# Layer A's cache copies one by one in the attention stages, and GpSimd's subtraction ahead of the next pair's weight sums

## The chip, the cores and the metric

The kernel runs on one core of one Trainium2 chip. The metric is the device time in microseconds (us), the median of the runs of one program. All data are float32 and lie in HBM before and after.

## The reference, cut to what matters

One inference step of a decoder trunk of two layers, for a prompt group (1024 tokens) and a sample group (8 sequences of 4 new tokens). Layer A, the first, multiplies the normalised input by one wide matrix `w_in_a` and runs dilated window attention in three groups, 4 heads each, beside attention into 256 memory tokens; layer B is a gated DeltaNet. The sample group keeps caches: of each group's keys and values the oldest 4 tokens are dropped where the window is full, and the 4 new ones appended. For the change only this counts:

```python
kc = jnp.concatenate([kbuf, k], axis=1)
vc = jnp.concatenate([vbuf, v], axis=1)
keep = min(win, L + T)
return o, lse, kc[:, L + T - keep:], vc[:, L + T - keep:]
```

So most of each new cache is a plain copy of the old one. For groups 1 and 2 (512 cached tokens, 4 heads of 128) these are four tensors, k and v of each, with 8 sequences of about 1 MB.

## The kernel before, in words

**Tasks.** The projection of layer A is made in 24 pairs of 128-column blocks of `w_in_a` (`SIDES`, six pairs for each of 4 heads). A pair is worked off by two tasks, one for each part of the tokens (`SUBS`: 272 and 256 columns), so there are 48 tasks; task t belongs to pair t // 2, and odd tasks are a pair's second half. A task is seven products of eight matmuls (`product`, L878): a scheme that gets four block products out of seven, from sums and differences of weights and of tokens. The weights' sums are made by GpSimd, four for each pair (`weight_sums(pair, ns)`, L1314, 128x512 each): the first overwrites half of the right block by left minus right, the second gives wS2, the third wS4, the fourth wS1. TensorE waits for the second ahead of a task's third product (i = 2), for the third ahead of i = 3, for the fourth ahead of i = 6. ScalarE and VectorE read the products out of PSUM (`evacuate`: L1046, L1049, L1052, L1062, L1065 on ScalarE, L1134, L1140, L1144, L1152, L1155 on VectorE). Between VectorE's step of i = 3 and its last step, i = 6 (L1152), GpSimd subtracts once for each task (L1334, `beside` with i = 4), and VectorE's last step waits for that (`pr_pool`).

**Weights.** Blocks of 128 columns, 512 KB each, lie in a ring of four slots (`Ring`, L136), two pairs. SyncE loads a block when the slot's old block is used up (`ring.used`), that is after the pair before last. TensorE waits for a pair's two loads ahead of its first product, GpSimd ahead of its first sum.

**Stages.** Behind the first four tasks (0 to 3) come 16 attention stages, s = 4h + g for head h and group g (g = 3 is the memory attention). Each stage has steps of its own: transposes (L915), scores (L930), transposed probabilities and values (L951, L954), softmax on VectorE (L1171, L1176, L1182, L1183) and ScalarE (L1087). The matmuls of three tasks are laid between them by `segments()`, in fixed shares: stage s has tasks 3s + 4 to 3s + 6, as far as there are any. All engines follow the same written order (`ended`, `stage_ends`). At stage g = 3 GpSimd also combines the three groups (`combined`, L1345 to L1349), called behind `beside` of task 12h + 14, i = 4.

**GpSimd's order.** For an odd task it issues the first three sums of the next pair at i = 3, the subtraction of the running task at i = 4, and the fourth sum at i = 6; for an even task only the subtraction. GpSimd works in order, so each waits for what stands ahead.

**Cache copies.** `copy_cache` (L302) issues four transfers from HBM to HBM on GpSimd's software queue, for two sequences each (2032 KB, or 2 MB where nothing is dropped). It is called at the start of stages 0, 4, 8 and 12, for one tensor each: 16 transfers in layer A's attention (L305). Eight small ones of group 0 come behind layer A (L2947). Only the end of the kernel waits for them all (L3101). Beside them SyncE issues the weight loads, the stores of new keys and values (L793 to L798), and the way of the groups' partial outputs to HBM and back (L814 to L821), all on the hardware queue.

Of the kernel before, what the change touches and what calls it, by code (L numbers as in the profile page):

```python
# [18 lines left out]
NB, DT = 8, 4  # L19
# [86 lines left out]
def after(eng, sem, value):  # L106

    if not isinstance(value, int) or value > 0:
        eng.wait_ge(sem, value)
# [34 lines left out]
def build(nc, ins, outs):  # L144
# [46 lines left out]
    NPAIR = len(SIDES) * H  # L191
# [107 lines left out]
    const_tp, const_sp, tab_in, mats_in = (nc.alloc_semaphore(n) for n in ("const_tp", "const_sp", "tab_in", "mats_in"))  # L299
    NTAB = 3 + H  # L300

    def copy_cache(pool, src, dst, n, drop):  # L302

        for b in range(0, NB, 2):
            pool.dma_start(dst[0, b:b + 2, 0:n - drop].rearrange("b t h e -> b (t h e)"),  # L305
                           src[0, b:b + 2, drop:n].rearrange("b t h e -> b (t h e)")).then_inc(copies, 16)
    NCOPY = 6 * NB // 2


    def part_in(k, part_):  # L310
# [54 lines left out]
    def tables_copied(pool):  # L365

        pool.wait_ge(tab_out, 32)
        pool.dma_start(toep, toep_rows.unsqueeze(1).to_broadcast([3 * H, P, 3 * P])).then_inc(tab_copied, 16)

    def sample_tables_in(pool):  # L370

        nc.gpsimd.memset(b2[:, :, :], NEG).then_inc(b2_set, 1)
        for h in range(H):
            pool.dma_start(bias_s[h * NS:(h + 1) * NS].rearrange("p g c -> p (g c)"),
                           sampb[h].unsqueeze(0).to_broadcast([NB, DT, 6 * P])).then_inc(tab_in, 16)

    def tables_in(pool):

        pool.wait_ge(b2_set, 1)
        pool.wait_ge(tab_copied, 16)  # L380
        pool.dma_start(b01[:, :, :], bass.AP(toep.tensor, P - 1, [[3 * P - 1, P], [P * 3 * P, 2 * H], [1, 256]])
                       ).then_inc(tab_in, 16)
        for r in range(2):
            pool.dma_start(b2[64 * r:64 * r + 64, :, 64 * r:64 * r + 64],
                           bass.AP(toep.tensor, 2 * H * P * 3 * P + 63,
                                   [[3 * P - 1, 64], [P * 3 * P, H], [1, 64]])).then_inc(tab_in, 16)
# [4 lines left out]
    @block.sync  # L391
    def _(sp):
        def x_load(n):
            sp.dma_start(xs[0:rows_in(n), n], load_in(n)).then_inc(x_in[n], 16)

        sp.dma_start(mats[:, 0:1, :], c_mats[:, 0:P].rearrange("p (m c) -> p m c", c=P)).then_inc(id_in, 16)
        x_load(XT)
        x_load(XT + 1)
        ring.load(sp, 2)
        sp.wait_ge(ring.loaded[0], 16)  # L400
        x_load(0)
        sp.dma_start(wb, norm_w[0].unsqueeze(0).to_broadcast([P, D])).then_inc(w_in, 16)
        x_load(1)
        ring.load(sp, 3)
        sp.wait_ge(rel_set, 1)
        sp.dma_start(relx[0:NBUCKET, :], rel_bias).then_inc(rel_in, 16)
        sp.dma_start(c_tp, c_toep).then_inc(const_tp, 16)
        x_load(2)
        x_load(3)
        ring.load(sp, 4)  # L410
        sp.dma_start(c_sp, c_samp).then_inc(const_sp, 16)
        x_load(4)
        x_load(5)
        ring.load(sp, 5)
        x_load(6)
        x_load(7)
        x_load(8)
        ring.load(sp, NMB + 2)
        sp.dma_start(mats[:, 1:, :], c_mats[:, P:].rearrange("p (m c) -> p m c", c=P)).then_inc(mats_in, 16)
        ring.load(sp, NMB + RING)  # L420
        sp.wait_ge(ev_a, 2)
        sp.wait_ge(ev_v, 2)
        sp.dma_start(memT_kept, memT_in).then_inc(memT_out, 16)
        sp.wait_ge(mem_tev, 8)
        mem_rows_out(sp, 0)
# [203 lines left out]
    for n in range(NPRE, len(loads)):  # L629
        a, i, kv = loads[n]  # L630
# [659 lines left out]
    @block.gpsimd  # L1290
    def _(pool):
        own = Chain(nc, pool, "pool_a")

        def weight_sums(pair, ns):

            x = (B0 + 2 * pair) % RING
            left, right = ring.slots[:, x, :, :], ring.slots[:, x + 1, :, :]
            before = NPROD * (2 * pair - 1)
            for n in ns:
                if n == 0:  # L1300
                    ring.wait(pool, B0 + 2 * pair)
                    ring.wait(pool, B0 + 2 * pair + 1)
                    v = right[:, 0:KH, :], left[:, 0:KH, :], right[:, 0:KH, :], ALU.subtract
                elif n == 1:
                    after(pool, pr_done, before + 3)
                    v = wS2, right[:, KH:KD, :], right[:, 0:KH, :], ALU.subtract
                elif n == 2:
                    after(pool, pr_done, before + 4)
                    v = wS4, left[:, KH:KD, :], wS2, ALU.subtract
                else:  # L1310
                    after(pool, pr_done, before + 7)
                    v = wS1, wS2, left[:, 0:KH, :], ALU.add
                after(pool, w_sums, 4 * pair + n)
                nc.gpsimd.tensor_tensor(*v).then_inc(w_sums, 1)  # L1314

        def token_rest(half):

            lo, hi = SUBS[half]
            pool.wait_ge(tok_sums, 2 * half + 2)
            v = hT[:, 0:KH, HALF + lo:HALF + hi]  # L1320
            nc.gpsimd.tensor_tensor(v, v, hT[:, 0:KH, lo:hi], ALU.subtract).then_inc(tok_rest, 1)
            four = lambda y: y.rearrange("p (a b) c -> p a b c", b=2)
            nc.gpsimd.tensor_tensor(tok_f[:, :, :, lo:hi], four(hT[:, KH:KD, lo:hi]), four(tok_e[:, :, lo:hi]),
                                    ALU.subtract).then_inc(tok_rest, 1)

        def beside(t, i):

            pair, n = t // 2, SUBS[t % 2][1] - SUBS[t % 2][0]
            if i == 3 and t % 2 and pair + 1 < NPAIR:
                weight_sums(pair + 1, (0, 1, 2))  # L1330
            if i == 4:
                pool.wait_ge(pr_dve, 4 * t + 2)
                pool.wait_ge(pr_act, 4 * t + 3)
                nc.gpsimd.tensor_tensor(w1s1[:, 0:n], w1s1[:, 0:n], u3[:, 0:n], ALU.subtract).then_inc(pr_pool, 1)  # L1334
            if i == 6 and t % 2 and pair + 1 < NPAIR:
                weight_sums(pair + 1, (3,))

        def combined(h):

            pool.wait_ge(comb_w, 2 * h + 2)  # L1340
            after(pool, t_read, EBASE[4] * h)
            if not h:
                pool.wait_ge(mem_out, 32)
            w = lambda g: wcomb[:, 2, g * NT:(g + 1) * NT].unsqueeze(2).to_broadcast([P, NT, E])
            own(nc.gpsimd.tensor_tensor(ocomb[:, :, :], og[0][:, :, 0:E], w(0), ALU.mult))  # L1345
            own(nc.gpsimd.tensor_tensor(og[1][:, :, 0:E], og[1][:, :, 0:E], w(1), ALU.mult))
            own(nc.gpsimd.tensor_tensor(og[2][:, :, 0:E], og[2][:, :, 0:E], w(2), ALU.mult))
            own(nc.gpsimd.tensor_tensor(ocomb[:, :, :], ocomb[:, :, :], og[1][:, :, 0:E], ALU.add))
            nc.gpsimd.tensor_tensor(ocomb[:, :, :], ocomb[:, :, :], og[2][:, :, 0:E], ALU.add).then_inc(comb_o, 1)  # L1349

        weight_sums(0, range(4))
        tables_copied(pool)
        pool.wait_ge(tab_row, 9)
        token_rest(0)
        pool.wait_ge(normed, NT + 1)
        token_rest(1)
        sample_tables_in(pool)
        for t, i in ALL_FIRST:
            beside(t, i)
            if (t, i) == (1, 4):  # L1360
                tables_in(pool)
        for s in range(NSTAGE):
            h, g = s // 4, s % 4
            if g == 0:
                copy_cache(pool, *((ck1, sk1, 512, DT), (cv1, sv1, 512, DT), (ck2, sk2, 512, 0),
                                   (cv2, sv2, 512, 0))[h])
            for t, i in stage_ends(s):
                beside(t, i)
                if g == 3 and (t, i) == (12 * h + 14, 4):
                    combined(h)  # L1370
            if s == NSTAGE - 1:
                pool.wait_ge(sc_read, 8 * (NSTAGE - 1))
                for v in Z_small:
                    own(nc.gpsimd.memset(v, 0.0))
                for g in (0, 2):
                    own(nc.gpsimd.tensor_copy(spread(0, g), gathered(0, g, q_of[0](g))))
                combined(h)
        pool.wait_ge(comb_o, H)
        own(nc.gpsimd.memset(Z_wide, 0.0))
# [1672 lines left out]
    def _(sp):  # L3052
# [46 lines left out]
        for i, d in enumerate(dso):  # L3099
            sp.wait_ge(d, 16 * len(range(i, NQ, 3)))  # L3100
        sp.wait_ge(copies, 16 * NCOPY)  # L3101
        sp.wait_ge(en, 1)
# [539 lines left out]
```

## Time and profile before

| | |
|---|---|
| median of 3 runs | 2256.55 us (2255.39 to 2259.75) |
| the profiled execution | 2256.22 us, its span 2254.3 us |
| TensorE busy | 2158.5 us, 96% |
| VectorE, ScalarE, GpSimd busy | 934.9, 663.6, 455.5 us |
| layer A's attention stages | about 112 to 862 us |
| mean granted clock of TensorE | 0.985 of full speed |

Times in the trace count from the span's start. A wait is put down to what ended it; "issue" is a wait that ended by no instruction that the profile shows, a transfer's landing among them. "SPq" is SyncE's queue of DMA issues. PEld is TensorE's loading of weights, which runs beside its matmuls.

### The profile page before, as it was taken

How to read it: one execution, taken by the hardware profiler on the slowest of the kernel's cores; microseconds unless marked ns; L12 is line 12 of the kernel's file. 1: busy time of each engine (PE TensorE's matmuls, PEld its weight loads, DVE VectorE, ACT ScalarE, POOL GpSimd, SP SyncE). 2: the span in 40 equal slices, each digit the busy share in tenths (PEclk: the TensorE clock that was granted, in tenths of full speed). 3: DMA queues.
4: the chain of work that ended last, by engine and by line, in shares of the span. 5: the costliest groups of instructions: out<-in, count | busy, mean ns of one | idle time of the engine just before them, and what ended most of it. 6: DMA issues, size and time to landing. Idle time of an engine off the chain costs nothing. (4 is left out here: it accounts for less than half of the span.)

```text
span 2254.3 us, 46735 instructions
## 1 busy us (share of the span) xinstructions
PE 2158.5 (96%) x19630; PEld 1533.0 (68%) x19630; DVE 934.9 (41%) x2431; ACT 663.6 (29%) x1589; POOL 455.5 (20%) x642
## 2 busy tenths in 40 slices
PE   8999988996999699999999999999999999999998
PEld 6888867885888587554466676766766766665444
DVE  5243443342435244331235555555556323333252
ACT  3122211311131123221133444444444344452101
POOL 0521232131223121400032123223222010010000
PEclk9999998998999899999999999999999999999999
DMA  7442232215132327657411011001001141015451
GB/s 225 154 182 82 57 141 76 76 38 189 29 85 86 132 67 223 230 179 237 150 29 31 3 31 32 22 12 32 22 3 41 29 166 57 19 45 170 132 175 53
DMA packets 210278, 210.99 MB, mean 94 GB/s; under 512 B 14262, under 2 KB 181654, under 8 KB 209151
## 3 DMA queue, kind: packets, MB, share of 16 engines
q1 hardware_dynamic: 198070, 148.27, 22.0%
q0 software_dynamic: 12000, 59.73, 7.0%
q8 instruction: 158, 2.59, 0.5%
q14 instruction: 50, 0.40, 0.1%
HBM read 179.56 MB, written 68.23 MB: 110 GB/s over the span
## 5 line engine op out<-in xcount | busy, mean ns | idle before, releaser
L878 PE MATMUL bank<-arena 128*128 128x256 f32 (+1 forms) x2688 | 635.2, 387 | 58.0 <-issue 58.0
L878 PEld LDWEIGHTS bank<-arena 128*128 128x128 f32 x2688 | 496.0, 191 | 134.5 <-issue 59.1
L2083 PE MATMUL bank<-arena 128*128 128x352 f32 x1296 | 468.9, 473 | 0.1
L2083 PEld LDWEIGHTS bank<-arena 128*128 128x128 f32 x1296 | 213.8, 190 | 58.1 <-ACT arena L2304 0.6
L1314 POOL TENSOR_TENSOR arena<-arena 128x512 f32<-128x512 f32 x96 | 122.8, 1279 | 308.2 <-PE bank L878 162.5
L2795 PE MATMUL bank<-arena 128*128 128x352 f32 x576 | 176.4, 459 | 0.0
L3283 PE MATMUL bank<-arena 128*128 128x512 f32 x360 | 167.5, 599 | 0.0
L2141 PEld LDWEIGHTS bank<-arena 128*128 128x128 f32 x864 | 125.1, 191 | 36.7 <-issue 0.3
L2795 PEld LDWEIGHTS bank<-arena 128*128 128x128 f32 x576 | 106.6, 190 | 53.3
L2157 PEld LDWEIGHTS bank<-arena 32*32 32x32 f32 x7680 | 78.6, 105 | 87.4 <-issue 35.4
L2141 PE MATMUL bank<-arena 128*128 128x128 f32 x864 | 130.8, 277 | 0.2 <-ACT arena L2324 0.2
L1654 PE MATMUL bank<-arena 128*128 128x512 f32 x248 | 122.1, 607 | 1.7 <-DMA arena<-in_w_out_a 1.7
L2440 DVE SCALAR_TENSOR_TENSOR arena<-arena 128x512 f32<-128x512 f32 x144 | 116.0, 806 | 1.2
L3283 PEld LDWEIGHTS bank<-arena 128*128 128x128 f32 x360 | 64.4, 189 | 70.4 <-issue 70.4
L2157 PE MATMUL bank<-arena 32*32 32x16 f32 (+1 forms) x7680 | 96.5, 183 | 1.1 <-DVE arena L2526 0.7
L1152 DVE TENSOR_TENSOR arena<-bank,arena 128x272 f32<-128x272 f32 (+1 forms) x48 | 24.2, 504 | 162.9 <-POOL arena L1334 87.8
L915 PE MATMUL bank<-arena 128*128 128x128 f32 x396 | 79.9, 278 | 8.4 <-ACT arena L1087 7.2
L1334 POOL TENSOR_TENSOR arena<-arena 128x272 f32<-128x272 f32 (+1 forms) x48 | 31.3, 652 | 269.2 <-ACT arena L1052 245.9
L1160 DVE COPY arena<-bank 128x256 f32<-128x256 f32 (+1 forms) x208 | 78.7, 383 | 13.9 <-PE bank L915 13.9
L1087 ACT ACTIVATE arena<-arena 128x256 f32<-128x256 f32 (+1 forms) x128 | 59.7, 467 | 83.3 <-DVE arena L1176 76.3
L915 PEld LDWEIGHTS bank<-arena 128*128 128x128 f32 x396 | 53.7, 143 | 30.4 <-ACT arena L1087 8.4
L2705 POOL TENSOR_TENSOR arena<-arena 128x512 f32<-128x512 f32 x16 | 21.1, 1321 | 252.2 <-DVE arena L2480 252.2
(426 smaller groups left out, 2717.9 us busy)
## 6 DMA issues: line engine op xcount, KB each, us to landing
arena<-in_w_in_a SPq DMA_DIRECT2D x48, 512.0 KB, 5.6
arena<-in_w_in_b SPq DMA_DIRECT2D x40, 512.0 KB, 3.8
arena<-in_cache_win_k SPq DMA_DIRECT2D x48, 256.0 KB, 5.0
arena<-in_cache_win_v SPq DMA_DIRECT2D x48, 256.0 KB, 3.6
out<-arena SPq DMA_DIRECT2D x40, 256.0 KB, 3.4
arena<-in_w_mem_kv SPq DMA_DIRECT2D x16, 512.0 KB, 8.1
arena<-in_cache_mem_k SPq DMA_DIRECT2D x32, 256.0 KB, 4.0
arena<-in_cache_mem_v SPq DMA_DIRECT2D x32, 256.0 KB, 3.7
```

The costliest lines, as they stand in the source:

```text
L878: m = nc.tensor.matmul(o[:, 0:hi - lo], w, y, start=k == 0 and i in (0, 1, 3, 5), stop=k == KH - 1, skip_group_check=i in (2, 4, 6))
L915: m = nc.tensor.transpose(tB[e % 2][:, c * P:(c + 1) * P], src, ident)
L1087: nc.scalar.activation(pr[:, x % 2, c:256], sS[:, x % 2, c:256], ACT.Exp, bias=nm, accum_out=l).then_inc(p_done, 1)
L1160: nc.vector.tensor_copy(dst, tB[e % 2][:, lo:lo + w]).then_inc(t_read, 1)
L1314: nc.gpsimd.tensor_tensor(*v).then_inc(w_sums, 1)
L1654: i = nc.tensor.matmul(bank[BY0 + half][:, :], brT[:, k, n * P:(n + 1) * P], wo_a(k)[:, half * 512:(half + 1) * 512], start=j == 0, stop=j ...
L2083: m = nc.tensor.matmul(bank[j % 3][:, 0:PART], ring.slots[:, (B1 + b) % RING, k, :], part_in(k, part_), start=k == 0, stop=k == KD - 1)
L2141: m = nc.tensor.matmul(o[:, c * P:(c + 1) * P], l, r, start=True, stop=True)
L2157: m = nc.tensor.matmul(o[quarter(i), lo:lo + r.free_size()], l, r, start=True, stop=True)
L2440: x = nc.vector.scalar_tensor_tensor(out=dst, in0=src, scalar=cw, in1=dst, op0=ALU.mult, op1=ALU.add)
L2795: m = nc.tensor.matmul(bank[part_][:, 0:PART], ring.slots[:, (B2 + b) % RING, k, :], part_in(k, part_), start=k == 0, stop=k == KD - 1)
L3283: m = nc.tensor.matmul(bank[BY0 + half][:, :], brT[:, k, n * P:(n + 1) * P], wo_b(k)[:, half * 512:(half + 1) * 512], start=j == 0, stop=j ...
```

## The change

`copy_cache` takes the list of sequences. A new helper, `copy_part(pool, n)`, issues the n-th of the 16 transfers alone (n // 4 is the tensor, n % 4 the pair of sequences). The four calls at the starts of stages 0, 4, 8 and 12 are gone. Transfers 14 and 15 are issued in the first tasks, behind `beside(2, 4)` and `beside(3, 4)`; transfers 0 to 13 in stages 0 to 13, behind `beside(3 * s + 5, 4)`, the middle task of each stage. In `beside`, the first three sums of the next pair move from i = 3 to i = 4, behind the running task's subtraction. What is computed, and the bytes that are copied, are the same.

```diff
-    def copy_cache(pool, src, dst, n, drop):
-
-        for b in range(0, NB, 2):
+    def copy_cache(pool, src, dst, n, drop, bs=range(0, NB, 2)):
+
+        for b in bs:
             pool.dma_start(dst[0, b:b + 2, 0:n - drop].rearrange("b t h e -> b (t h e)"),
                            src[0, b:b + 2, drop:n].rearrange("b t h e -> b (t h e)")).then_inc(copies, 16)
     NCOPY = 6 * NB // 2
+
+    def copy_part(pool, n):
+
+        src, dst, drop = ((ck1, sk1, DT), (cv1, sv1, DT), (ck2, sk2, 0), (cv2, sv2, 0))[n // 4]
+        copy_cache(pool, src, dst, 512, drop, (n % 4 * 2,))
...
         def beside(t, i):
 
             pair, n = t // 2, SUBS[t % 2][1] - SUBS[t % 2][0]
-            if i == 3 and t % 2 and pair + 1 < NPAIR:
-                weight_sums(pair + 1, (0, 1, 2))
             if i == 4:
                 pool.wait_ge(pr_dve, 4 * t + 2)
                 pool.wait_ge(pr_act, 4 * t + 3)
                 nc.gpsimd.tensor_tensor(w1s1[:, 0:n], w1s1[:, 0:n], u3[:, 0:n], ALU.subtract).then_inc(pr_pool, 1)
+                if t % 2 and pair + 1 < NPAIR:
+                    weight_sums(pair + 1, (0, 1, 2))
             if i == 6 and t % 2 and pair + 1 < NPAIR:
                 weight_sums(pair + 1, (3,))
...
             beside(t, i)
             if (t, i) == (1, 4):
                 tables_in(pool)
+            if (t, i) in ((2, 4), (3, 4)):
+                copy_part(pool, 12 + t)
         for s in range(NSTAGE):
             h, g = s // 4, s % 4
-            if g == 0:
-                copy_cache(pool, *((ck1, sk1, 512, DT), (cv1, sv1, 512, DT), (ck2, sk2, 512, 0),
-                                   (cv2, sv2, 512, 0))[h])
             for t, i in stage_ends(s):
                 beside(t, i)
+                if (t, i) == (3 * s + 5, 4) and s < 14:
+                    copy_part(pool, s)
                 if g == 3 and (t, i) == (12 * h + 14, 4):
                     combined(h)
```

## Rows read from the trace of the kernel before

**Rows 1.** The page: busy time, share of the span and instructions of each engine.
```profile
PE 2158.5 (96%) x19630; PEld 1533.0 (68%) x19630; DVE 934.9 (41%) x2431; ACT 663.6 (29%) x1589; POOL 455.5 (20%) x642
```

**Rows 2.** The waits: who waited for whom; us in total, times, longest.
```profile
DVE arena L1152 <- POOL arena L1334: 87.8, 6, 25.0
...
PE bank L878 <- issue: 58.0, 3, 19.4
...
PE bank L915 <- ACT arena L1087: 7.2, 6, 1.6
```

**Rows 3.** Timeline, first long wait: start, length, instruction, [idle before it].
```profile
348.00 1.24 PE L878 MATMUL bank<-arena 128*128 128x272 f32 x2 [19.32 <-issue]
348.04 4.08 POOL L1314 TENSOR_TENSOR arena<-arena 128x512 f32<-128x512 f32 x3 [37.49 <-issue]
```

**Rows 4.** Timelines of GpSimd and SyncE ahead of it: the copies and the loads.
```profile
112.31 2.44 POOL L305 DMA_DIRECT2D out<-in_cache_win_k  x4
...
299.30 2.40 POOL L305 DMA_DIRECT2D out<-in_cache_win_v  x4
...
307.73 38.59 SPq L136 DMA_DIRECT2D arena<-in_w_in_a  x4
```

**Rows 5.** Weight loads: head 1's, head 0's (issue time ns, landing us), all 48 (KB, landing).
```profile
L136 SPq DMA_DIRECT2D arena<-in_w_in_a x2: 448/17045/33642, 307.7 to 308.2; - x2
...
DMA to landing us min/median/max: 38.5/39.1/39.7
...
L136 SPq DMA_DIRECT2D arena<-in_w_in_a x2: 391/7189/13987, 140.6 to 141.1; - x2
...
DMA to landing us min/median/max: 18.9/19.4/19.9
...
arena<-in_w_in_a SPq DMA_DIRECT2D x48, 512.0 KB, 5.6
```

**Rows 6.** DMA queues from 302 to 343 us: packets, MB, share of 16 engines.
```profile
q0 software_dynamic: 416, 8.06, 47.6%
q1 hardware_dynamic: 1022, 0.50, 4.4%
```

**Rows 7.** Windows, heads' starts: length, busy (instructions) by engine, clock, DMA, GB/s.
```profile
123.65:154.94 31.29, 31.29 (x160) 27.00 (x159) 12.76 (x33) 6.02 (x20) 6.34 (x6) 1.00 0.53 217
309.89:363.24 53.35, 34.03 (x163) 28.85 (x162) 14.05 (x36) 7.09 (x22) 6.28 (x7) 0.81 0.44 167
...
sum 191.26, PE 133.29 PEld 113.52 DVE 54.92 ACT 27.30 POOL 25.18; mean PE 33.32 PEld 28.38 DVE 13.73 ACT 6.82 POOL 6.30
```

**Rows 8.** The same view of 5 us within TensorE's long wait.
```profile
335.00:340.00 5.00, 0.00 (x0) 0.00 (x0) 0.00 (x0) 0.00 (x0) 0.00 (x0) 0.50 0.49 210
```

**Rows 9.** Timelines: loads of stages 0 and 2, task 8, subtraction of 13, task 14.
```profile
140.65 14.42 SPq L136 DMA_DIRECT2D arena<-in_w_in_a  x2
...
175.04 4.29 PE L878 MATMUL bank<-arena 128*128 128x272 f32 x18
...
217.74 17.04 SPq L136 DMA_DIRECT2D arena<-in_w_in_a  x4
...
260.21 0.63 POOL L1334 TENSOR_TENSOR arena<-arena 128x256 f32<-128x256 f32 x1 [1.58 <-ACT arena L1052]
...
264.05 4.29 PE L878 MATMUL bank<-arena 128*128 128x272 f32 x18
```

**Rows 10.** Timelines round task 15 on GpSimd, ScalarE, VectorE and TensorE.
```profile
293.38 4.15 POOL L1314 TENSOR_TENSOR arena<-arena 128x512 f32<-128x512 f32 x3
...
294.94 0.36 ACT L1062 ACTIVATE arena<-bank 128x224 f32<-128x224 f32 x1 [2.58 <-PE bank L878]
...
298.22 0.39 DVE L1152 TENSOR_TENSOR arena<-bank,arena 128x224 f32<-128x224 f32 x1 [4.30 <-POOL arena L1334]
...
299.29 0.71 PE L951 MATMUL bank<-arena 128*128 128x128 f32 x4 [0.97 <-DVE arena L1160]
```

**Rows 11.** Groups by line: all weight sums, up to 900 us.
```profile
L1314 POOL TENSOR_TENSOR arena<-arena 128x512 f32<-128x512 f32 x96 | 122.8, 1279 | 308.2 <-PE bank L878 162.5 <-issue 143.6
```

## The prediction

> **What bounds the kernel now.** I read the page first: TensorE is busy for 96% of the span [rows 1], so only time in which it stands still, or runs slowly, can be won. The waits say where it stands: of all its idle time on work of layer A one group is large, three waits of the projection matmuls (L878) with 58.0 us together, 19.4 us the longest, put down to "issue", which here means something that is no engine. VectorE waits for GpSimd's subtraction (L1334) up to 25.0 us [rows 2].
>
> The timeline round the first of the three shows a chain. TensorE and GpSimd start again within 0.04 us of each other, at 348.00 and 348.04, after 19.32 and 37.49 us [rows 3]. Both wait there for the same thing: the two weight blocks of pair 9, TensorE for task 18, GpSimd for `weight_sums`. GpSimd had issued four cache copies from 299.30 on; SyncE issued the weight blocks at 307.7 [rows 4]. They landed 38.5 to 39.7 us after issue, where such a load has a median of 5.6; in head 0, where the load at 140.6 came 28 us after the copies at 112.31, it took 18.9 to 19.9 [rows 4, 5]. In 302 to 343 us the software queue (the copies) moved 8.06 MB in 416 packets and the hardware queue (the loads and two stores) 0.50 MB in 1022 [rows 6]: hardly one block's worth. So the load stands behind the copies until they are done, about 41 us for four, 10.3 us for one.
>
> What one such stall costs is read from the same stretch of four heads, from the subtraction of task 4 (16, 28, 40) to that of task 6 (18, 30, 42). Head 0, without a stall, needs 31.29 us; all four together 191.26 [rows 7]. The excess is 191.26 - 4 x 31.29 = 66.1 us, 22.03 for each of the three heads: 19.3 idle and 2.7 of slower work. The clock was granted at 0.50 (1.2 GHz) while TensorE stood idle, and TensorE's busy time in the stretch rose from 31.29 to 34.03 [rows 7, 8].
>
> **Part 1, the copies.** The same 16 transfers are issued, two in the first tasks (tasks 2 and 3), then one in each of stages 0 to 13, right behind the subtraction of the stage's middle task (t = 3s + 5); where that task is odd, behind three weight sums too. At the point where a head begins nothing is issued any more, so the load of pair 9 (15, 21) at the head's start meets no copy: stage 3's copy goes out behind task 14's subtraction, one task (about 16 us) after task 13's at 260.21 [rows 9], and needs some 10 us; the load comes at 307.7. All three stalls go: **-66.1 us**. GpSimd pays the same 16 issues of 0.6 us (four in 2.40 us [rows 4]) in its own idle time; at task 14 the issue stands ahead of `combined`, which waits longer than that for VectorE anyway.
>
> Which loads now meet a copy? In stages with s even. Stage 0: the load is issued at 140.65, the copy goes out behind task 5's sums at about 143.5; in the worst case the load waits the copy's whole 10.3 us and then takes its 5.6, so 16 us, and lands by 157. TensorE wants it for task 8 at 175.04: 18 us to spare. Stage 2: the last blocks are issued at about 234 (the end of a run of four that began at 217.74), the copy goes out at about 236, they land by 251, and TensorE wants them at 264.05 [rows 9]: 13 us to spare. The other heads repeat this. I cost these at nothing; if the cover were gone, it would be rival 1. Loads of tasks 2 and 3 have a whole pair of tasks as well.
>
> **Part 2, subtraction first.** Before, an odd task's subtraction stood in GpSimd's queue behind the first three sums of the next pair, one of which waits for a load. Now it stands ahead. Two effects. With loads in time it matters once per head, at task 15 (27, 39), where `combined` makes GpSimd late: the three sums ran from 293.38 for 4.15 us, VectorE waited 4.30 us and began at 298.22, and TensorE, whose attention step waits for VectorE, lost 0.97 us at 299.29 and 0.19 a little later. With the subtraction first it ends at 294.0; VectorE then waits for ScalarE's copies (294.94 and one more, ending about 295.4) instead and begins 2.8 us earlier, more than TensorE was short [rows 10]. **-1.2 us** in each of three heads, **-3.5 us**. Task 47 has no sums behind it.
>
> The other side: the sums are now later by the subtraction and by what they could do ahead of it. The sum that TensorE needs first is the second, for the third product of the next task. At task 13: subtraction from 260.21 to 260.84, two sums of 1.27, done at 263.4, the third at 264.7, the fourth at 265.9. Task 14's products start at 264.05; two of them, 16 matmuls of the 18 in 4.29 us, come first, so the third starts at about 267.9, the fourth near 270 [rows 9]. 4.5 us to spare; in the first tasks, which run without attention between them, I estimate 3 to 4 us: eight matmuls at 0.238 us make 1.9 us a product, four products lie between product 4 and the sum's use, 7.6 us, and the reading, the subtraction and two sums need about 4. Nothing waits for the fourth sum before the seventh product. The tables of tasks 0 and 1 (issued behind task 1's subtraction) go out 3.8 us later, still ahead of stage 0, where they are used first. Cost: 0, bounded below by nothing and above by rival 3.
>
> What was behind the stalls otherwise? TensorE's next waits are those for the softmax, 7.2 us in six waits [rows 2]; they stay. The work behind layer A moves forward as a whole.
>
> **Sum.** The profiled execution took 2256.2 us (span 2254.3). 2256.2 - 66.1 - 3.5 = 2186.6; the median shown is 0.3 above that execution, so 2187.
>
> **Rival 1, the delay comes back in pieces.** The same bytes are still moved beside the loads, by the same 16 engines. If one copy holds a load as long as four did (a load is held by turns, not by bytes), the load of stage 0 lands 39 us after 140.65, at 179.7, 4.6 us late for 175.04, and that of stage 2 at 273, 9 us late. Four of the first and three of the second (stage 14 has no copy): 45 us back, 2232. Against it stands head 0: its load met the last 13 us of the copies and took 19.4, so it came free when they ended [rows 5]. Partly so, it gives anything down to the forecast. The Trainium skill, "DMA: Bandwidth & Descriptors", section "Issuing engines are not separate DMA queues", is on this rival's side: transfers run on the same 16 engines and interleave whoever issues them, so spreading saves no transfer time. The trace agrees with that for the bytes; what counts here is only which load stands beside them.
>
> **Rival 2, it does not do what it says.** If the loads were late by something other than the copies (SyncE's own queue), only part 2 is won: 2252.7, within 0.2%. Against it: the load without copies near it has 5.6 us.
>
> **Rival 3, slower: TensorE waits for sums.** At the 23 handovers from an odd task to the next pair, two sums must be done 7.7 us after the subtraction's start (260.21 to 267.9). Sums of 1.27 us leave 4.5. It costs TensorE time from (7.7 - 0.6)/2 = 3.5 us a sum on, and undoes the gain of 69.6 when each handover loses 3.0 us, at 5.0 us a sum. At 6 us it would be 23 x 4.9 - 69.6 = +43, so 2299. Against it: 96 sums have a mean of 1.279 us, also where they run beside VectorE [rows 11]. The Trainium skill, "SBUF — State Buffer", section "Who interferes with whom", speaks for it: a VectorE instruction with two SBUF inputs contends with a reading GpSimd instruction, and one of the two blocks. The rows above bear out no such factor for the sums.
>
> **How the numbers follow.** Forecast 0.86, rival 1 in full or in part 0.08, rival 2 0.03, rival 3 0.03. Low end: the softmax waits go too (7.2), 2179.4, so 2179. High end: one of the three stalls stays or comes back in small pieces, 2186.6 + 22.0 = 2208.6, so 2209; that takes in the smaller half of rival 1. A measurement of this kernel can tell about 0.2% (4.5 us) from no change. Faster: forecast and rival 1, 0.94; same: rival 2, 0.03; slower: rival 3, 0.03.
>
> **What would show it.** Right: no wait of L878 for "issue" on TensorE; the clock without the three stretches at 0.50; all four heads' stretches near 31.3 us; VectorE's wait for L1334 down from 87.8 us to a few; copies as 16 single issues; loads beside a copy landing within 16 us, others in about 5.6. The term of 3.5 is wrong if TensorE still idles at task 15. Wrong as a whole: a load lands 30 us or more after issue (rival 1), the three waits stay with single copies in flight (rival 2), or TensorE waits for L1314 at L878 (rival 3).

## The result: slower by 150 us, and the profile after

The changed kernel takes 2406.2 us (median of 4 runs, 2397.3 to 2421.6) against 2256.0: ratio 1.067, interval 1.061 to 1.073. The forecast was 2187.

The page of the changed kernel (busy time, as [rows 1]; its line numbers are up to 6 higher than before), and TensorE's waits of its first 1000 us (who for whom; us, times, longest), as [rows 2]:

```profile
PE 2174.0 (90%) x19630; PEld 1543.9 (64%) x19630; DVE 941.5 (39%) x2431; ACT 663.9 (28%) x1589; POOL 455.9 (19%) x642
```
```profile
PE bank L883 <- ACT arena L1051: 112.3, 3, 37.6
PE bank L883 <- issue: 63.5, 3, 23.9
PE bank L920 <- ACT arena L1092: 27.2, 6, 12.0
```

L883 is the projection matmul. Its waits for loads ("issue") did not go: there are three again, at other places (tasks 8, 34 and 46). New are three waits of 37 us, and the softmax's share grew (30.1 us in the whole span, 7.2 before). Idle time of the three kinds: 205.9 us against 65.2, so 140.7 more; TensorE's busy time is 15.5 us longer; the instructions are the same, and the mean granted clock is 0.953 against 0.985. Together 156.2, and the spans differ by 156.4.

The copies themselves are the key. The changed kernel's line L305 (issue time on GpSimd in ns, then us from issue to landing):

```profile
L305 POOL DMA_DIRECT2D out<-in_cache_win_v x8: 630/642/671, 95.8 to 939.7; - x8
L305 POOL DMA_DIRECT2D out<-in_cache_win_k x8: 630/630/653, 145.0 to 803.8; - x8
...
DMA to landing us min/median/max: 18.4/41.9/43.5
```

A copy alone takes as long as four together did, 42 us, not 10. (All copies count up one semaphore, so of two that overlap only the later landing can be read; the 18.4 is the first of such a pair.) A window of the changed kernel inside the first of the long waits, with one copy and one reload in flight (columns as in [rows 7]):

```profile
330.00:340.00 10.00, 0.00 (x0) 0.00 (x0) 0.00 (x0) 0.00 (x0) 0.00 (x0) 0.50 0.12 52
```

The DMA share is 0.12 of 16 engines, which is two, at 52 GB/s; with four copies it was 0.50, eight engines, at 210 [rows 8]. The other fourteen have nothing to do, and still TensorE stands. The same place in the timelines of GpSimd, SyncE, VectorE and TensorE, with the landing time of the reload L826 (the partial outputs of group 2, back from HBM):

```profile
309.14 0.63 POOL L305 DMA_DIRECT2D out<-in_cache_win_k  x1
...
311.98 0.37 SPq L826 DMA_DIRECT2D arena<-part  x1
...
DMA to landing us min/median/max: 40.3/40.3/40.3
...
352.29 0.17 DVE L1214 TENSOR_TENSOR arena<-arena 128x8 f32<-128x8 f32 x1 [39.45 <-DMA arena<-part]
...
353.62 1.22 PE L883 MATMUL bank<-arena 128*128 128x256 f32 x2 [37.43 <-ACT arena L1051]
```

The reload is issued 3 us behind the copy of stage 3 and lands 40.3 us later, just after the copy. VectorE waits for it to weigh the three groups, ScalarE for VectorE, TensorE for ScalarE. What moved in that time, by queue (columns as in [rows 6]), from 312 to 318 and from 318 to 348 us:

```profile
q1 hardware_dynamic: 1822, 0.93, 55.8%
q0 software_dynamic: 4, 0.26, 10.8%
...
q0 software_dynamic: 24, 1.56, 12.0%
q1 hardware_dynamic: 24, 0.01, 0.1%
```

In the first 6 us the hardware queue moved 0.93 MB, which is fourteen sixteenths of the reload and one weight block (520 and 512 KB). In the next 30 us it got 24 packets, as many as the copy, but the copy's hold about 64 KB each and its own about 0.5 KB. So what lies on the fourteen free engines passes at once, and the rest waits on the copy's two engines.

The longer softmax waits have the same cause. Two of them, of 12.0 and 11.8 us, are 23.8 of the 30.1 us. VectorE's waits there are for a store of partial outputs (L819), issued at 227 with the copy of 202.98 in flight and landing after up to 18.7 us; before, none of these stores took more than 2.5 us:

```profile
DVE arena L1176 <- DMA part<-arena: 28.3, 2, 14.2
```

The first wait for a load is at task 8: the blocks issued at 140 land after up to 47.9 us, behind the copy of 145.0, and TensorE loses 15.75 us at 188.43.

### The profile page after: what moved, and what is told of

Same layout as the page of the kernel before. It is cut to its first block and busy times, and to the rows that moved or that the text cites. A ratio compares the mean times of both kernels' runs of the same rounds, so it can differ in the third digit from the quotient of the medians.

```text
span 2410.7 us, 46735 instructions
## 1 busy us (share of the span) xinstructions
PE 2174.0 (90%) x19630; PEld 1543.9 (64%) x19630; DVE 941.5 (39%) x2431; ACT 663.9 (28%) x1589; POOL 455.9 (19%) x642
## 5 line engine op out<-in xcount | busy, mean ns | idle before, releaser
L883 PE MATMUL bank<-arena 128*128 128x256 f32 (+1 forms) x2688 | 649.3, 393 | 175.8 <-ACT arena L1051 112.3
L883 PEld LDWEIGHTS bank<-arena 128*128 128x128 f32 x2688 | 505.4, 194 | 257.4 <-ACT arena L1051 113.5
L920 PE MATMUL bank<-arena 128*128 128x128 f32 x396 | 80.4, 279 | 31.3 <-ACT arena L1092 30.1
```

The source lines that it names most:

```text
L883: m = nc.tensor.matmul(o[:, 0:hi - lo], w, y, start=k == 0 and i in (0, 1, 3, 5), stop=k == KH - 1, skip_group_check=i in (2, 4, 6))
L920: m = nc.tensor.transpose(tB[e % 2][:, c * P:(c + 1) * P], src, ident)
```

## The experiments

Theory A: a narrow copy occupies few engines for 42 us, and whatever is spread over all 16 is held by its share on those. Rival B: the new order of GpSimd's sums is the loss.

**e1, e2: the two halves of the change alone.** e1 has the new order with the copies at the heads' starts; e2 the copies of the changed kernel with the old order:

```diff
# e1, against the kernel before
-            if i == 3 and t % 2 and pair + 1 < NPAIR:
-                weight_sums(pair + 1, (0, 1, 2))
             if i == 4:
...
+                if t % 2 and pair + 1 < NPAIR:
+                    weight_sums(pair + 1, (0, 1, 2))
```

> Only the order on GpSimd is changed, the copies stay in fours at the heads' starts. Theory A (the loss comes from the copies alone): the three stalls of 19.4 us stay, the 1.2 us at tasks 15, 27 and 39 go: 2252.5, ratio 0.998. Theory B (the loss of 150 us comes from the weight sums, now behind the subtraction): near 2400, with waits of the projection matmuls for L1314.

> Only the copies are moved, one into each stage; GpSimd's order stays as before. Theory A: near the changed kernel, 2400 to 2420, or a little more, since VectorE now also waits for a subtraction that stands behind sums that wait for a late load. Theory B: about 2190, the stalls of before gone and no new ones.

e1: 2257.6 us, ratio 0.9999 (0.9990 to 1.0008). e2: 2363.0, ratio 1.048 (1.046 to 1.049). The loss comes with the copies; the order alone is worth nothing there. Why nothing, when 3.5 us were forecast, is in e1's waits:

```profile
PE bank L878 <- issue: 64.6, 3, 22.0
PE bank L915 <- ACT arena L1087: 7.2, 6, 1.6
```

TensorE's three waits of 0.97 us (L951) are gone, but the waits for the load grew from 58.0 to 64.6 us: TensorE comes earlier to a load that lands no earlier. e2 is 43 us faster than the changed kernel, against the expectation of about the same. Its reloads L826 land in at most 4.8 us and it has no wait of 37 us; it pays 108.0 us in eight waits for loads instead, and 42.3 for the softmax:

```profile
PE bank L883 <- issue: 108.0, 8, 24.1
PE bank L920 <- ACT arena L1092: 42.3, 8, 12.8
```

**e3: the same copies, wide.** Only the shape of the access pattern differs (64 pieces of 16 KB outermost, where it was the 2 sequences):

```diff
+            rows_ = lambda v: v.rearrange("b t h e -> b (t h e)")
+            if n == 512:
+                rows_ = lambda v: v.rearrange("b t h e -> b (t h e)").rearrange("b (x n) -> x b n", x=64)
-            pool.dma_start(dst[0, b:b + 2, 0:n - drop].rearrange("b t h e -> b (t h e)"),
-                           src[0, b:b + 2, drop:n].rearrange("b t h e -> b (t h e)")).then_inc(copies, 16)
+            pool.dma_start(rows_(dst[0, b:b + 2, 0:n - drop]), rows_(src[0, b:b + 2, drop:n])).then_inc(copies, 16)
```

> The changed kernel, but each copy's access pattern has 64 pieces of 16 KB outermost instead of the 2 sequences: same bytes, same places. Theory A1 (a transfer whose outermost dimension is 2 runs on 2 of the 16 DMA engines: the DMA share with one copy alone in flight is 0.11 to 0.13, and 50 GB/s): the copies now land in 5 to 12 us at a share near 1.0, all long waits of TensorE go, 2185 to 2195. Rival A2 (one software transfer is held to 50 GB/s by its queue or by HBM, whatever its shape): still about 42 us to landing and about 2400.

2188.3 us, ratio 0.970 (0.968 to 0.971). The page of e3, its copies of layer A (L308), a window with one alone in flight, and the first of TensorE's waits:

```profile
PE 2151.5 (98%) x19630; PEld 1529.1 (70%) x19630; DVE 938.0 (43%) x2431; ACT 663.3 (30%) x1589; POOL 455.3 (21%) x642
...
DMA to landing us min/median/max: 8.2/8.8/10.0
...
187.00:192.00 5.00, 5.00 (x27) 4.34 (x26) 1.99 (x7) 1.51 (x4) 0.00 (x0) 1.00 0.96 361
...
PE bank L922 <- ACT arena L1094: 7.2, 6, 1.6
```

The same bytes at the same places, now at a share of 0.96 and 361 GB/s, land in 8.8 us; TensorE waits for no load. The same bytes in another shape: 218 us apart. The shape changes two things, the outermost count and the size of the pieces; e9 tells them apart.

**e4: wide, but still in fours at the heads' starts** (the kernel before with the same edit).

> The kernel before, with the same 64 pieces outermost and the four copies still at the heads' starts. Theory A1: 8.3 MB over all 16 engines take about 20 us instead of 41; the load of 307.7, issued 8 us behind them, lands by about 325, ahead of TensorE's need at 329: the three stalls go nearly or all, 2190 to 2200. Rival A2: as before, 2256. Rival A3 (where the copies stand decides, not how wide they are): stalls of 19.4 us stay, 2256.

2207.4 us, ratio 0.978 (0.977 to 0.980), 19 us above e3 and 7 above the range expected: the three waits are still there, 3.8 us the longest. The first of them, the copies and the load in e4:

```profile
297.27 2.37 POOL L308 DMA_DIRECT2D out<-in_cache_win_v  x4
...
306.56 21.92 SPq L136 DMA_DIRECT2D arena<-in_w_in_a  x4
...
DMA to landing us min/median/max: 22.0/22.5/23.1
...
330.47 1.25 PE L880 MATMUL bank<-arena 128*128 128x272 f32 x2 [3.80 <-issue]
```

Four wide copies take 27 us, not 20, at 310 GB/s, and hold the load for 22. From 312 to 320 us, with the load issued at 306.56, e4's queues moved:

```profile
q0 software_dynamic: 171, 2.49, 97.7%
q1 hardware_dynamic: 171, 0.08, 3.3%
```

So 16 KB pieces on all engines hold a load too; both parts are needed, wide and one at a time.

**e5: no copies** (the 16 copies left out, so their four outputs too).

> The changed kernel without the 16 copies of groups 1 and 2 (their outputs are left out, and the end waits for the eight others only). This is the floor for any placement. If the wide copies cost TensorE nothing: the time of the run with 64 pieces, 2188, within 3 us. If they still cost something through slower loads: 2175 to 2184.

2187.3 us, ratio 0.969 (0.968 to 0.970). e3 is 1 us above this floor: wide single copies cost next to nothing.

**e6: wide and single, old order** (e3 with the weight sums back at i = 3).

> One wide copy in each stage, but the old order on GpSimd (three sums ahead of the subtraction). Theory A with part 2 of the prediction: 3.5 us slower than the same with the new order, 2188.3 + 3.5 = 2191.8, TensorE's waits of 0.97 us at L956 three times. Rival (the order is worth nothing even without stalls): 2188.

2190.6 us, ratio 0.971 (0.969 to 0.972), 2.3 us above e3. The intervals overlap, but the trace of e6 has the waits that e3 lacks, as [rows 10]:

```profile
PE bank L958 <- DVE arena L1167: 2.9, 3, 1.0
```

**e7: two narrow copies at once, in stages g = 0 and 1 only.**

```diff
-                if (t, i) == (3 * s + 5, 4) and s < 14:
+                if (t, i) == (3 * s + 5, 4) and s < 14 and g < 2:
                     copy_part(pool, s)
+                    if s + 2 < 14:
+                        copy_part(pool, s + 2)
```

> The changed kernel with the narrow copies, but two at once in stages g = 0 and g = 1 and none in g = 2 and g = 3 (stages 12 and 13 have one each). Theory (each narrow copy is 42 us on two engines of its own; the 112 us of waits for ScalarE L1051 come from the way of the partial outputs to HBM and back at stages 2 and 3, which meets a copy): each copy still lands in 42 us at a DMA share of 0.25, the waits of 37 us go, those for loads (64 us) stay or grow: 2270 to 2320. Rival (the delay grows with the bytes in flight): copies of 84 us, and no gain over 2406.

2284.2 us, ratio 1.013 (1.009 to 1.017). In e7 the reloads land in at most 4.7 us and no wait of 37 us is left. The pair at 202 us (the last landing, 42.2, is the one that can be read: 2 MB do not move in the 2.2 us of the first), a window with two in flight, and TensorE's waits:

```profile
DMA to landing us min/median/max: 2.2/22.2/42.2
...
230.00:240.00 10.00, 5.08 (x27) 4.13 (x25) 1.27 (x4) 0.39 (x1) 0.67 (x1) 0.87 0.25 107
...
PE bank L920 <- ACT arena L1092: 45.6, 8, 14.1
PE bank L883 <- issue: 42.8, 2, 25.8
```

Twice the bytes, the same 42 us, at 0.25 of the engines: one narrow copy, two and four all take 42 to 44 us. The waits for loads fell to 42.8 us where 64 or more were expected, and those for the softmax grew to 45.6; VectorE waits 44.4 us for the stores of partial outputs there. The run is 79 us faster than e2, whose reloads are free too. That fewer stages with a copy are cheaper is argued from this, since the copies also stand elsewhere.

**e8: a ladder that wasn't one.** Three tensors were cut to one sequence and 4, 8 and 16 contiguous pieces:

```diff
-        copy_cache(pool, src, dst, 512, drop, (n % 4 * 2,))
+        if n // 4 == 3:
+            return copy_cache(pool, src, dst, 512, drop, (n % 4 * 2,))
+        for b in (n % 4 * 2, n % 4 * 2 + 1):
+            piece = lambda v: v.rearrange("t h e -> (t h e)").rearrange("(x n) -> x n", x=(4, 8, 16)[n // 4])
+            pool.dma_start(piece(dst[0, b, 0:512 - drop]), piece(src[0, b, drop:512])).then_inc(copies, 16)
```

> The changed kernel with the copies of three tensors cut to one sequence each, 1 MB, with 4, 8 and 16 pieces outermost; the fourth tensor stays as it is, 2 sequences outermost. Theory (the outermost count is the number of engines, each moving some 25 GB/s): landing in 10.4, 5.2 and 2.6 us and some 2 more, 42 for the fourth. Rival (the queue is held to 50 GB/s): 21 us for all three.

A miss. The three rungs came out alike: the sixteen copies of the first two tensors, in pairs, have a median of 7.4 and 7.2 us, those of the third 7.2; the fourth tensor's 39.7. The window with 4 pieces outermost shows every engine at work:

```profile
186.00:190.00 4.00, 4.00 (x22) 3.43 (x21) 2.04 (x6) 0.80 (x3) 0.00 (x0) 1.00 1.00 390
```

Contiguous pieces, however they are counted in the source, seem to be joined to one run and cut anew. That is argued from the alike times, no more. The run gave something else: only four narrow copies were left (tasks 2 and 3, stages 12 and 13), and it takes 2215.6 us, 27 above e3, with one wait, behind the copy of 699.38:

```profile
PE bank L887 <- issue: 23.7, 1, 23.7
```

**e9: the ladder with pieces that cannot be joined** (each copy one sequence in 64 pieces of 16 KB, the outermost 2, 4, 8 or 16 at a stride of one piece):

```diff
-        copy_cache(pool, src, dst, 512, drop, (n % 4 * 2,))
+        for b in (n % 4 * 2, n % 4 * 2 + 1):
+            x = (2, 4, 8, 16)[n // 4]
+            piece = lambda v: v.rearrange("t h e -> (t h e)").rearrange("(y x n) -> x y n", x=x, y=64 // x)
+            pool.dma_start(piece(dst[0, b, 0:512 - drop]), piece(src[0, b, drop:512])).then_inc(copies, 16)
```

> The changed kernel, each copy cut to one sequence (1 MB), always in 64 pieces of 16 KB, with 2, 4, 8 and 16 pieces outermost for the four tensors, at strides that cannot be merged into one run. Theory (the outermost count is the number of DMA engines, 25 GB/s each, whatever the size of the pieces): landing in 21, 10.4, 5.2 and 2.6 us, plus up to 2 us; the two copies of a slot go side by side for 2, 4 and 8. Rival (small pieces are what made the wide copies fast): about 4 to 7 us for all four.

Four windows of e9, for 2, 4, 8 and 16 outermost, each with a pair of 1 MB copies in flight; the last two columns are the share and GB/s:

```profile
190.00:200.00 10.00, 10.00 (x53) 8.83 (x53) 4.32 (x12) 1.96 (x7) 0.00 (x0) 1.00 0.26 109
375.00:380.00 5.00, 5.00 (x28) 4.43 (x27) 2.42 (x7) 0.87 (x3) 0.00 (x0) 1.00 0.50 210
558.00:562.00 4.00, 4.00 (x22) 3.47 (x21) 1.87 (x6) 0.91 (x2) 0.00 (x0) 1.00 0.86 295
702.00:705.00 3.00, 3.00 (x17) 2.53 (x16) 0.91 (x2) 0.41 (x2) 0.00 (x0) 1.00 1.03 406
```

The share is twice the outermost count over 16 (two copies), until all engines work: 4, 8 and some 14 of them at 0.86, all at 1.03. The pairs land by 23.9, 13.5, 9.1 and 9.3 us. The pieces are of one size in all four, so width decides, not the size. Per engine it is 27 GB/s at two outermost and 26 at four, as the narrow copy's 26 (52 GB/s on two) with pieces of 64 KB. The whole kernel takes 2188.1 us, ratio 0.970 (0.968 to 0.972): copies of 23.9 us in a stage cost TensorE nothing, those of 42 do. They met hardly any load: no weight block of layer A takes more than 6.9 us to land in e9, or 6.6 in e3. So e9 does not show how a load fares that stands beside them.

**e10: the narrow copies of stage g = 3 one task later.**

```diff
-                if (t, i) == (3 * s + 5, 4) and s < 14:
+                if (t, i) == (3 * s + (6 if g == 3 else 5), 4) and s < 14:
```

> The changed kernel with its narrow copies; only the copies of the stages g = 3 go out one task later (task 12h + 15 instead of 12h + 14). Theory (112 us of TensorE's waits are three reloads of partial outputs, issued 3 us behind a copy, each held for 40 us): the reload now lands in about 4 us, VectorE's wait at L1214 (118 us) and TensorE's for L1051 (112 us) go; the copy then stands beside the next head's weight loads, which gives some back, up to 3 times 20 us: 2300 to 2360. Rival (the reload is late whatever stands beside it): no gain.

2359.8 us, ratio 1.045 (1.042 to 1.049). The reload, and TensorE's waits, in e10:

```profile
DMA to landing us min/median/max: 3.8/4.0/5.2
...
PE bank L883 <- issue: 130.7, 7, 24.1
PE bank L920 <- ACT arena L1092: 19.3, 7, 12.2
PE bank L883 <- ACT arena L1051: 5.8, 3, 2.7
```

The 112.3 us are down to 5.8, so they were the reload held by the copy. More than half of it comes back as waits for weight loads, 130.7 us instead of 63.5. With a narrow copy in flight most of the time, moving it only chooses the victim. The 43 us between e2 and the changed kernel are such a choice: in the changed kernel three copies go out 3 to 4 us ahead of a reload, in e2 the same three go out 13 us behind it.

## Why the prediction was wrong, point by point

**The step that failed** is the term "10.3 us for one", got by dividing 41 us by four copies. It takes for granted that four copies share one resource in turn. They ran side by side, each on two engines of its own; one alone takes 41.9. The row that could have told was on the table: the four copies used 47.6% of 16 engines [rows 6], in the window 0.50 [rows 8], at a steady 210 GB/s for 41 us. Four transfers that leave half of the engines idle all this time are not sharing all of them. The Trainium skill, "DMA: Bandwidth & Descriptors", section "Why a DMA increments its semaphore by 16 and not by 1", states the rule: the slowest dimension that is not 1 sets how many engines a transfer uses, the largest number up to 16 that divides it on both sides. Here it is the two sequences. The shares of 0.12, 0.25 and 0.50 for one, two and four copies, and e9's ladder, agree with it. e8's contiguous pieces agree only if they were joined first, which is argued.

**A second row was read wrongly.** "Hardly one block's worth" in 41 us [rows 6] was taken for a load that stands still until the copies are done. Of its 1022 packets 678 had passed by 315 us (0.33 MB, half of one block and the two stores), as they would on the half of the engines that the copies left free; from 325 to 340 us the kernel before moved 48 packets on each queue:

```profile
q0 software_dynamic: 48, 3.12, 49.9%
q1 hardware_dynamic: 48, 0.02, 0.5%
```

**From it followed the rest.** Sixteen copies of 42 us are 672 us in attention stages that lasted 750 before, so a copy is in flight most of the time and reaches from one stage into the next. "They land by 157" was up to 188, and the "18 us to spare" of stage 0 became the wait of 15.75 at task 8. The load of stage 2, with "13 us to spare", landed within 6.5 us in head 0, and TensorE waited for it in no head. The other two waits, 23.8 and 23.9 us, are for loads of an odd stage (tasks 34 and 46), which the prediction had meet no copy. "I cost these at nothing" was 63.5 us. I also listed only weight loads as what a copy could meet. The dearest victim was the reload of partial outputs: 112.3 of the 140.7 us of added idle time. The stores ahead of it, which the softmax waits for, make 23.8 more.

**Rival 1 was the right mechanism, with 0.08 and a size of 2232.** It was set aside because head 0's load "came free when they ended", which a load held by four side-by-side copies does too: that row could not tell the two apart. Its size was wrong for the same omission. It counted weight loads only; the held reloads alone are the 112 us. Its words "by turns, not by bytes" are what the packets show, 24 against 24.

**What held.** That the copies cause the three stalls (e5: without them there are none). The price of the stalls and the sum: with copies that are as short as assumed, 8.8 us, the change gives 2188.3, where 2187 was forecast. That the sums behind the subtraction cost nothing: e3, with the new order, is 2.3 us faster than e6 with the old one, and TensorE waits for no weight sum in e3, e1 or the changed kernel, so rival 3 never showed. Rival 2 fell with e5. **Part 2** was put at 3.5 us; e6 against e3 gives 2.3, with the 2.9 us of L958 gone and the 1.2 us in four waits of the next step unchanged. While the stalls were there it was worth nothing (e1).

## What to carry to other kernels

Before a large transfer is spread in time, read how wide it is: bytes over time for one alone, and the DMA share while only it is in flight. A transfer on two engines holds everything that is spread over sixteen, as long as it lasts, at a DMA share that looks idle. Give it an outermost dimension of 16 or a multiple of it (64 in e3, 16 in e9's last tensor), then issue one at a time: e3 beats both kernels, 2188.3 us against 2256 and 2406.

## What the runs showed that I had not expected

Two queues that meet on an engine take turns packet by packet, whatever the packets hold: 24 against 24 in the changed kernel, 48 against 48 in the kernel before, 171 against 171 in e4. By bytes the held one gets very little, in e4 0.08 MB against 2.49. A weight block is some 64 packets of 0.5 KB for each engine. A turn took about 2.5 us beside the narrow copy and 0.75 us beside e4's wide ones, so by turns alone the block would need 160 or 48 us: an estimate from these counts, longer than the copies last in both cases. A run with single narrow copies in pieces of 16 KB (e11) gave no result, and smaller pieces were not tried.

A fix on the path ahead of a fixed landing is worth nothing: e1's 3 us were swallowed whole by the load. And the runs of some kernels with narrow copies spread widely, the changed kernel's and e7's over 24 us, e10's over 16, but e2's over 2 and e3's over 4; no run shows why.
